# Decay rows of two mixers: spread by DMA through DRAM and formed on GpSimd, instead of by matmuls on TensorE

## The reference

```python
# first block: state space mixer, 16 heads (chunks of 64 in the reference)
seg = a_cs[..., :, None] - a_cs[..., None, :]          # a_cs: running sum of dt * a
decay = exp(where(causal, seg, -inf))
y = (cb * decay) @ (x * dt)                            # cb = C B^T, per group of 8 heads
# beside it a gated linear recurrence, both gated, projected, then an FFN
# second block: gated delta rule, 4 heads, chunks of 64
diff = gc[..., :, None] - gc[..., None, :]             # gc: running sum of g in a chunk
L = (beta k) k^T * exp(diff)   (strictly lower);   a_qk = q k^T * exp(diff)   (lower)
qg = q * exp(gc);   d_last = exp(gc at the chunk's end)
# beside it three more branches (spatial gate, sliding window, memory), merged by gates
```

## Time and profile before

| what | value |
|---|---|
| median of three runs | 1000.08 us (998.61 to 1000.84) |
| the profiled execution | 1000.26 us, of it span 998.5 us |
| TensorE busy | 95% of the span |
| VectorE, ScalarE, GpSimd busy | 62%, 50%, 44% |
| mean granted clock of TensorE | 0.966 |
| DMA | 143.37 MB, 44% of the 16 engines' time |

### The profile page before, as it was taken

One profiled execution on the slowest core, in us unless ns is written; L12 is line 12 of the kernel. 1 busy time (PEld: TensorE's weight loads), 2 busy tenths in 40 slices (PEclk: granted clock), 3 DMA queues, 4 the chain that ended last, 5 costly groups with the idle time before them and its releaser, 6 DMA issues.

```text
span 998.5 us, 17155 instructions
## 1 busy us (share of the span) xinstructions
PE 945.6 (95%) x6754; PEld 877.0 (88%) x6754; DVE 619.4 (62%) x1160; ACT 502.4 (50%) x784; POOL 434.6 (44%) x344
## 2 busy tenths in 40 slices
PE   6879999989998999999997989999999999999995
PEld 6879988979997999999996989999999777778884
DVE  6797644966867855645557787653656543655564
ACT  5556667645343755656554557333445423445541
POOL 3444222557363665565554424221322322445652
PEclk9999999979997999999999999998999989999998
DMA  8435432436451555565553345432322322346541
GB/s 322 155 122 179 149 107 85 134 120 226 151 179 61 188 189 188 172 189 189 178 183 105 101 145 194 128 108 76 131 85 85 108 84 83 115 147 196 193 151 43
DMA packets 39684, 143.37 MB, mean 144 GB/s; under 512 B 4402, under 2 KB 4532, under 8 KB 39348
## 3 DMA queue, kind: packets, MB, share of 16 engines
q1 hardware_dynamic: 39604, 142.27, 43.6%
HBM read 141.21 MB, written 1.05 MB: 142 GB/s over the span
## 4 chain that ended last, share of the span: by engine, by line
PE 78%; DVE 15%; ACT 4%; issue 2%; POOL 1%; DMA 1%; SPq 0%; ACTq 0%; DVEq 0%
PE bank L535 29%; PE bank L530 16%; PE bank L531 16%; PE bank L532 16%; DVE t_arena L1638 5%; DVE t_wl L1624 3%; DVE t_arena L1630 2%; DVE t_sm L1635 2%; PE bank L538 2%; ACT t_wh L1167 1%; ACT t_arena L1172 1%; DVE t_arena L1844 1%; DVE t_arena L1634 1%; ACT t_br L1172 1%; DVE t_sm L1634 1%
## 5 line engine op out<-in xcount | busy, mean ns | idle before, releaser
L2271 POOL TENSOR_TENSOR t_wl<-t_raw,t_wh 128x384 fp32r<-128x384 f32 x260 | 365.9, 1413 | 489.6 <-ACT t_wh L1167 489.6
L530 PE MATMUL bank<-t_hh,t_wh 128*128 128x256 f32 x1208 | 353.0, 292 | 12.4 <-DVE t_wl L1624 9.0
L531 PE MATMUL bank<-t_hl,t_wh 128*128 128x256 f32 x1208 | 344.6, 285 | 0.0
L532 PE MATMUL bank<-t_hh,t_wl 128*128 128x256 f32 x1208 | 344.4, 285 | 0.0
L1624 DVE TENSOR_TENSOR t_wl<-t_raw,t_wh 128x640 fp32r<-128x640 f32 x260 | 244.6, 946 | 152.3 <-ACT t_wh L1167 151.2
L1167 ACT ACTIVATE t_wh<-t_raw 128x1024 fp32r<-128x1024 f32 x260 | 272.2, 1056 | 129.1 <-PE bank L532 93.9
L530 PEld LDWEIGHTS bank<-t_hh,t_wh 128*128 128x128 f32 x1208 | 234.6, 194 | 17.9 <-DVE t_wl L1624 10.7
L531 PEld LDWEIGHTS bank<-t_hl,t_wh 128*128 128x128 f32 x1208 | 234.8, 194 | 0.3
L532 PEld LDWEIGHTS bank<-t_hh,t_wl 128*128 128x128 f32 x1208 | 234.4, 194 | 0.0
L530 PE MATMUL bank<-t_br,t_wh 128*128 128x256 f32 x424 | 124.8, 294 | 10.7 <-DVE t_br L1638 8.4
L531 PE MATMUL bank<-t_br,t_wh 128*128 128x256 f32 x424 | 123.4, 291 | 0.0
(11 more groups left out here) (139 smaller groups left out, 1023.4 us busy)
## 6 DMA issues: line engine op xcount, KB each, us to landing
t_raw<-in_ws SPq DMA_DIRECT2D x260, 512.0 KB, 4.2
t_x<-in_xin SPq DMA_DIRECT2D x4, 256.0 KB, 5.8
t_bd<-in_bd SPq DMA_DIRECT2D x1, 1024.0 KB, 11.5
t_arena<-in_mem SPq DMA_DIRECT2D x1, 1024.0 KB, 5.0
out<-t_arena SPq DMA_DIRECT2D x4, 256.0 KB, 2.4
t_arena<-in_post SPq DMA_DIRECT2D x1, 512.0 KB, 5.5
t_con<-in_con SPq DMA_DIRECT2D x1, 384.0 KB, 6.5
t_arena<-in_masks SPq DMA_DIRECT2D x1, 320.0 KB, 9.5
```

Of the source, the lines that this page charges most:

```text
L530: e.matmul(o, wh, xh, start=first, stop=False, skip_group_check=True)
L531: e.matmul(o, wh, xl, start=False, stop=False, skip_group_check=True)
L532: return e.matmul(o, wl, xh, start=False, stop=last, skip_group_check=True)
L2271: e.tensor_tensor(WL[q % NS][:, LOW:1024], RAW[q % NR][:, LOW:1024], WH[q % NS][:, LOW:1024].bitcast(F), SUB).then_inc(*lo2.now(q))
```

## The change

The rows no longer go through TensorE. `acs` is written to a DRAM tensor `decay` and read back into all 128 partitions (`ACS`, 16 rows of 256, 2.1 MB in all, in the place of `BR`). GpSimd forms row plus negated column, held at most at zero, for 256 and 128 columns per head, into one of four buffers `DEC`; ScalarE's `Exp` becomes one instruction of 384 columns in place; the causal mask is multiplied into `CBT` once. In the delta rule `beta`, `gc` and `eg` go through `gates2` into `BG` (12 rows of 256, 1.6 MB in all), GpSimd forms differences plus mask, and VectorE reads `BG` where it read PSUM. The four DMAs stand on SP's queue among the fetches. The copies `identR`, `ACR` and the mask `maskS` are gone, `INCL` is made at tick 12 instead of in the second block, and `kk` moves a tick earlier and uses three banks in turn.

```diff
@@ sp_program, in the loop over the fetches q @@
+                if q == 20:
+                    e.wait_ge(*d_dt.of("acs"))
+                    e.dma_start(decay, acs).then_inc(s_decay[0], 16)
+                if q == 23:
+                    e.wait_ge(s_decay[0], 16)
+                    e.wait_ge(*unit.of(LAST["xbc5"]))
+                    e.dma_start(ACS, decay.partition_broadcast(P)).then_inc(s_decay[1], 16)
+                if q == LAST["dnq4"] + 1:
+                    e.wait_ge(*d_rw.of("beta"))
+                    e.wait_ge(*a_rw.of("eg"))
+                    e.dma_start(gates2[0], ROW[0:4, 0, :]).then_inc(s_gates[0], 16)
+                    e.dma_start(gates2[1:3].rearrange("i h t -> h i t"), ROW[4:8, 1:3, :]).then_inc(s_gates[0], 16)
+                if q == LAST["dnq5"] + 3:
+                    e.wait_ge(s_gates[0], 32)
+                    e.dma_start(BG, gates2.rearrange("i h t -> (i h) t").partition_broadcast(P)).then_inc(s_gates[1], 16)
@@ pe_program, ssd_lane @@
-                for h in range(16):
-                    yield from walk.until(T_HEAD + h)
-                    ps = PB[3 + h % 2]
-                    sel = identR[0:16, h:h + 1].to_broadcast([16, 128])
...
-                    mm(ps[:, 0:128], identB[:, :], maskS[:, :], True, False)
-                    for w in range(2):
-                        mm(ps[:, 0:T], sel, ACR[:, w, :], False, w == 1)
-                    mm(ps[:, T:384], identB[:, :], maskS[:, :], True, False)
-                    for w in range(2):
-                        m = mm(ps[:, T:384], sel, ACR[:, w, 128:256], False, w == 1)
-                    m.then_inc(*p_ssd.now("seg", h))
-                    if h % 2 == 1 and h > 1:
-                        y_pair(h // 2 - 1)
-                yield from walk.until(42)
-                y_pair(7)
+                for t in range(8):
+                    yield from walk.until(T_HEAD + 2 * t + 3 - t // 7)
+                    y_pair(t)
@@ pe_program, dn_lane @@
                     yield from walk.until(170 + 2 * h)
-                    for i in range(2):
-                        mm(PB[3][:, 128 * i:128 * i + 128], identB[:, :], maskD[:, :], i == 0, False)
-                    mm(PB[3][:, 0:T], sg, ROW[0:8, 1, :], False, True)
-                    mm(PB[3][:, T:512], sg, ROW[0:8, 2, :]).then_inc(*p_dn.now("seg", h))
-                    mm(PB[4][:, 0:T], sb_, ROW[0:8, 0, :]).then_inc(*p_dn.now("beta", h))
-                    yield from walk.until(171 + 2 * h)
                     for hf in range(2):
                         for w in range(2):
-                            m = mm(PB[5][...], k_[...], (k_, q_)[w][...])
+                            m = mm(PB[3 + h % 3][...], k_[...], (k_, q_)[w][...])
@@ act_program, ssd_lane @@
                 for h in range(16):
                     yield from walk.until(T_HEAD + h)
-                    e.wait_ge(*p_ssd.of("seg", h))
...
-                    act(dec[:, 0:T], ps[:, 0:T], ACT.Exp, bias=cols_dt[:, 2, h:h + 1])
-                    act(dec[:, T:384], ps[:, T:384], ACT.Exp, bias=cols_dt[:, 3, h:h + 1]).then_inc(*a_ssd.now("exp", h))
+                    e.wait_ge(*g_ssd.of("seg", h))
+                    act(DEC[h % 4], DEC[h % 4], ACT.Exp).then_inc(*a_ssd.now("exp", h))
@@ act_program, dn_lane @@
-                    yield from walk.until(171 + 2 * h)
-                    e.wait_ge(*p_dn.of("seg", h))
-                    for hf in range(2):
-                        act(ET[:, hf, h, :], PB[3][:, 128 * hf:128 * hf + 128], ACT.Exp,
-                            bias=ngc[:, hf, 4 + h:5 + h]).then_inc(*a_dn.now("dec", h, hf))
+                    yield from walk.until(169 + 2 * h)
+                    e.wait_ge(*g_dn.of("seg", h))
+                    act(ET[:, :, h, :], ET[:, :, h, :], ACT.Exp).then_inc(*a_dn.now("dec", h))
@@ dve_program, ssd_lane @@
+                tt(INCL[:, :], cn("strict"), ident, ADD).then_inc(*d_const.now("incl"))
                 for g in range(2):
...
-                    e.tensor_copy(CBT[:, g, :], PB[4][:, 0:384]).then_inc(*d_ssd.now("cb", g))
+                    for i in (0, 2):
+                        tt(CBT[:, g, 128 * i:128 * i + 128], PB[4][:, 128 * i:128 * i + 128], INCL[:, :], MUL)
+                    e.tensor_copy(CBT[:, g, 128:256], PB[4][:, 128:256]).then_inc(*d_ssd.now("cb", g))
@@ pool_program @@
+            def ssd_lane():
+                for h in range(16):
+                    yield from walk.until(T_HEAD + h)
+                    if h == 0:
+                        e.wait_ge(s_decay[1], 16)
+                        e.wait_ge(*d_dt.of("cols"))
+                    if h >= 4:
+                        e.wait_ge(*p_ssd.of("y", (h - 4) // 2))
+                    for i, sl in enumerate((slice(0, T), slice(T, 384))):
+                        m = e.tensor_scalar(DEC[h % 4][:, sl], ACS[:, h, 128 * i:T], cols_dt[:, 2 + i, h:h + 1], 0.0, ADD, MIN)
+                    m.then_inc(*g_ssd.now("seg", h))
+                yield
+
+            def dn_lane():
+                for h in range(4):
+                    yield from walk.until(168 + 2 * h)
...
+                    for hf in range(2):
+                        e.tensor_scalar(ET[:, hf, h, :], BG[:, 4 + h, 128 * hf:128 * hf + 128], ngc[:, hf, 4 + h:5 + h], None,
+                                        ADD).then_inc(*g_dn.now("diff", h, hf))
+                    for hf in range(2):
+                        e.wait_ge(*g_dn.of("diff", h, hf))
+                        m = tt(ET[:, hf, h, :], ET[:, hf, h, :], maskD[:, :], ADD)
+                    m.then_inc(*g_dn.now("seg", h))
+                yield
+
+            walk.lanes = [ffn_lane(), ssd_lane(), lru_lane(), rows_lane(), dn_lane()]
```

More of the change, by code:

```diff
@@ L142, in constants @@
     return [np.concatenate([out[n] for n in names], 1).astype(np.float32)
-            for names in ([n for n, _ in CON], ("ssm", "sw", "seg"))]
+            for names in ([n for n, _ in CON], ("sw", "seg"))]
 class Tally:
@@ L290, in dn_bank, with build_program @@
     return 3 + (DN_AT[name] + 1) % 3
-def build_program(nc, ws, par, con, masks, bd, rows, swt, xin, min_, post2, out):
+def build_program(nc, ws, par, con, masks, bd, rows, swt, xin, min_, post2, decay, gates2, out):
     ctx = ExitStack()
@@ L313, in build_program @@
         s_sp, s_out, s_post = sem("s_sp"), sem("s_out"), sem("s_post")
+        s_decay, s_gates = [sem(f"s_decay{i}") for i in range(2)], [sem(f"s_gates{i}") for i in range(2)]
         s_x = [sem(f"s_x{i}") for i in range(4)]
@@ L344, in build_program @@
         NW2 = SM[:, 352:364].rearrange("p (a b) -> p a b", a=3)
-        maskS = sb("maskS", [P, 128], BF)
         maskW = sb("maskW", [P, 384], BF)
-        maskD = sb("maskD", [P, 128], BF)
+        maskD = sb("maskD", [P, 128])
         identB = sb("identB", [P, 128], BF)
-        identR, ACR = sb("identR", [P, P], R), sb("acr", [16, 2, T], R)
         INCL = sb("incl", [P, P], BF)
         PX, PW = sb("px", [P, 1024]), sb("pw", [P, 768])
-        MSK = ar(0, 640)
+        MSK = ar(0, 512)
         XBC = ar(0, 12, T)
@@ L365, in build_program @@
         CBT = ar(76, 2, 384)
-        DEC = ar(79, 3, 384)
+        DEC = [ar(79, 384), ARENA[:, 79 * 256 + 384:79 * 256 + 768], ar(82, 384), ar(88, 384)]
+        ACS = BR.rearrange("p a b -> p (a b)").bitcast(F).rearrange("p (h t) -> p h t", h=16)
+        BG = ar(78, 12, T)
         DTR = ar(84, 4, T)
@@ L695, in ssd_lane @@
                 e.wait_ge(*d_rs.of("ssd"))
-                e.wait_ge(*a_ssd.of("exp", 15))
+                e.wait_ge(*d_ssd.of("cb", 1))
                 for g in range(2):
@@ L1239, in ssd_lane @@
                 act(DTR[0:16, 1, :], DTR[0:16, 1, :], ACT.Exp, scale=-1.0).then_inc(*a_dt.now("exp"))
-                yield from walk.until(12)
-                e.wait_ge(*d_dt.of("acs"))
-                act(ACR[:, 0, :], acs, ACT.Copy).then_inc(*a_dt.now("acr"))
                 for h in range(16):
                     yield from walk.until(T_HEAD + h)
-                    ps, dec = PB[3 + h % 2], DEC[:, h % 3, :]
-                    e.wait_ge(*p_ssd.of("seg", h))
-                    if h == 0:
-                        e.wait_ge(*d_dt.of("cols"))
-                    if h >= 3:
-                        e.wait_ge(*p_ssd.of("y", (h - 3) // 2))
-                    act(dec[:, 0:T], ps[:, 0:T], ACT.Exp, bias=cols_dt[:, 2, h:h + 1])
-                    act(dec[:, T:384], ps[:, T:384], ACT.Exp, bias=cols_dt[:, 3, h:h + 1]).then_inc(*a_ssd.now("exp", h))
+                    e.wait_ge(*g_ssd.of("seg", h))
+                    act(DEC[h % 4], DEC[h % 4], ACT.Exp).then_inc(*a_ssd.now("exp", h))
                 yield from walk.until(43)
@@ L1414, in act_program @@
             h_parts("mix", SC1)
-            e.wait_ge(s_con, 16)
-            act(identR[:, :], ident, ACT.Copy).then_inc(*a_const.now("identR"))
             def gates(i):
@@ L1777, in ssd_lane @@
```

(13 more changed lines are left out.)

44 lines of the change are left out of this document (20 added, 24 removed).

## The result

The changed kernel is slower: 1019.02 us (median of 4 runs, 1012.23 to 1022.73) against 1000.46 for the kernel before beside it, a ratio of 1.018 with a 95% interval of 1.0125 to 1.0237. Timed a second time it came to 1016.41 against 998.07, 1.0192 (1.0168 to 1.0216). The prediction of 1002.7 had the direction, and its range ended at 1010: 9 us too early.

The account below looks back on a forecast made before the run. TensorE, busy for 95% of the span, was taken as the bound, with ScalarE and GpSimd taking turns in the mixer after the change. +10.3 - 6.8 + 0.8 - 1.7 = +2.6 us gave 1002.7 us, range 994 to 1010.

Parts of the forecast that it names:

- The loop: Mixer, each unit: high part, GpSimd's low part, differences, Exp, next high part wait in a closed ring; 5.56 us a unit.
- x: Mixer: time of GpSimd's two difference instructions per head, taken as 0.9 us, ends 0.62 and 1.25.
- +10.3: Mixer: total lateness in us summed over all heads, arriving at `gsum`; ends +6.1 and +15.5.
- some 3 us less: Mixer: how much the sum would fall at the skill page's best GpSimd rate, 0.58 us for 384 columns.
- the 17.8 us: Mixer: row matmuls taken from TensorE, 16 x 1.11 us, said to become idle time in front of the units.
- The start after the high part (0.08) and the low part (1.48): Mixer: hand-over from ScalarE's high part to GpSimd, 0.08 us, and mean time of GpSimd's low part, 1.48 us.
- The exclusion that the Trainium skill states: Mixer: two-SBUF-input VectorE instructions and GpSimd ones reading SBUF exclude each other; cited for the 1007.9 us rival, chance 0.2.
- `decay`: Copy through DRAM ahead of unit 23's fetch: hidden, cost 0, up to 2 us at the slow end.
- `gates2`: Gates' copy on SP's queue ahead of unit 168's fetch, waiting for `eg`: +0.8 us, ends 0 and 2.3.
- Delta rule: Four heads: 6.8 us of row matmuls saved, plus 1.7 us from one avoided clock fall (ends 0 and 5.0).
- The clock in the mixer: Rival: gaps lower TensorE's clock in the mixer, 7.1 us a unit, 22 us more, 1025 us; chance 0.06.
- The loop does not bind: Rival: in the mixer TensorE's time is won, heads 0 to 10 end 12 us earlier, 982 us; chance 0.07.

Follow-up runs that it names:

- thin differences: Changed kernel, but from head 4 on GpSimd forms only 2 columns per difference instruction and Exp has scale 0: 1004.79 us, ratio 1.0052.
- the mixer alone: Kernel before with only the mixer's part of the change, the delta rule left as it was: 1024.92 us, ratio 1.024.
- delta rule's part alone: Kernel before with only the delta rule's part of the change, gates' copies placed as in the change: 994.5 us, ratio 0.9953.
- GpSimd ahead: Changed kernel with GpSimd forming the mixer's differences one tick earlier, at tick 24+h: 977.95 us, ratio 0.9785.
- late copies: Kernels with the gates' writes and broadcast moved to 4 and 7 units behind dnq5; with differences a tick earlier 975.4 us, delta rule's part only 991.21 us.

## Why the prediction was wrong, by its own steps

**The loop: right. x: wrong, and it is nearly the whole miss.** The step that failed reads "I take x = 0.9, nearest to the casts", with 1.25 as the upper end. Measured: 1.83 undisturbed, and 2.69 and 2.68 beside VectorE's scans and low part (the pairs at 196.96 and 209.18 us). The 15 pairs of heads 1 to 15 add up to 29.2 us, where the sum has 15 x 0.9 = 13.5: 15.7 us more than the +10.3, 26.0, where the trace has 25.9 at `gsum` and 24.7 at unit 54. It holds in parts:
- Heads 0 to 11 take 71.1 us from `Exp` to `Exp` (112.01 to 183.12), 6.46 us each; 5.56 + 0.93 is 6.49.
- Head 11 to 12 takes 11.3 us against 9.25: +2.0, forecast +1.05 with an x too small by 0.93.
- Heads 12 to 14 take 12.2 against 6.47: +5.8, forecast +3.2 with two such x, of which one is too small by 0.94 and the other, beside the scans, by 1.79: +5.9.

Put into the same sum, the pairs of the thin differences give 26.0 - 14.8 = 11.2, where `gsum` came 11.2 us later and unit 54 10.3. So the mechanism of the forecast was right and one term of its sum was not. Its ends were taken from casts (of the three casts of 128 columns in that trace, 344, 478 and 877 ns, the shortest) and from a subtraction split in two, and neither is a bound for this operation: with one input it costs more than the two-input one, 1139 ns for 256 columns against a mean of 733 for `t_x<-t_x,t_arena` of the same width in the kernel before. Undisturbed, the difference between 256 and 128 columns is (1139 - 712) / 128 = 3.3 ns a column, and two columns take 0.29 us, nearly all of it fixed time. The Trainium skill (GPSIMD Engine Reference, 3.1) gives 1.8 cycles an element at best and 2.6 for a two-input addition. The 3.3 ns are more than both: at the 1.2 GHz of that section, an estimate, 4.0 cycles. The prediction's "some 3 us less" from the best rate does not come out of its own numbers either: 15 x (0.9 - 0.58) is 4.8.

**That the loss "arrives at `gsum`, for which TensorE waits already", and that the 17.8 us turn into idle time:** right. The loss of the mixer alone stays at +25.4 to the end.

**The start after the high part (0.08) and the low part (1.48):** right: 0.08 (114.21 to 114.29), and 1.48 on average from 110 to 190 us.

**The exclusion that the Trainium skill states (SBUF — State Buffer, Who interferes with whom):** the trace agrees at the low part, 1.65 us at 114.29 with VectorE's beside it against 1.03 at 195.95, and in the thin kernel, where two columns took 0.99 us instead of 0.29 while VectorE's low part of 0.82 us ran (136.03 us). Of the pairs of differences only two met such work (2.7 against 1.83), since VectorE waited for `Exp` as well: none up to head 12, 1.7 us of the miss in all.

**`decay`:** forecast 0 and right. The broadcast took 10.4 us to land, between my 5 and 17, the fetch of unit 23 behind it landed at 83.0 us, 2 us ahead of its high part, and units 23 to 30 are within 1 us of before in every kernel that has it.

**`gates2`:** forecast +0.8, ends 0 and 2.3; measured +5.6, +5.1 (delta rule's part alone) and +5.3 (GpSimd ahead), and 3.3 to 4.0 in the other four profiles with early copies (3.3 in the second one of the changed kernel). The wait was named rightly, and with it the late fetch. Two terms were missed. The loads of `swt` and `rows` stand at the same place of the same queue and put the fetch of 168 another 1.1 us back. And that fetch, the first of four issued together, landed 6.3 us after its issue and not 3 to 4.2. In the seven profiles its landing takes 4.05, 4.3, 4.5, 4.7, 5.8, 6.0 and 6.3 us, and the loss is 3.3, 3.6, 3.8, 4.0, 5.1, 5.3 and 5.6: the one follows the other. Why the landing varies so was not tried.

**Delta rule:** -6.8 for the row matmuls and -1.7 for the clock, 8.5; measured -9.5 to -9.6 in three profiles with this part (the first of the changed kernel among them) and -11.0 in eight. The three have one fall of the clock of 3.4 us left in the stage, the eight none, where the kernel before has 10.2 us at the lower level. So 3.4 us at that level cost 1.5, all 10.2 some 4.5, and about 6.5 are left for the matmuls. The step that failed here is "I count the first fall, a third of it, as avoided": two thirds were, or all. Ahead of the stage, from unit 168 to 180, a new fall takes some of it back, which was not forecast: 1.4 us in three of the four kernels with late copies, 0.2 in the changed kernel.

**The clock in the mixer (a rival with 0.06):** it did fall to 0.50, at gaps of 4.9 to 7.3 us, and set nothing: from 110 to 215 us ScalarE never waits for TensorE, and the loop alone accounts for the shift. The idle time was forecast as gaps of 1.6 us a unit, in front of most units; that was wrong. Until 190 us it comes in three pieces (7.3, 5.4 and 4.9 us), because TensorE's next task behind its lead is the recurrent unit's matmul, which waits for ScalarE's tanh and exp, queued behind the waiting `Exp`.

**The rivals.** "The loop does not bind" was given 982 us. The true one is beside it: the loop need not exist. I took the order of GpSimd's program as given, weighed whether it binds, and did not ask what one tick would change. Sum of the terms as measured: 24.7 + 1.2 + 5.6 - 9.5 = 22.0, and the span's difference is 22.4 us. The profiled execution is the slowest of its four; by the medians the difference is 18.6. The second profile has a shift of 16.2 at the end: 2.3 less at the fetch of 168, and 1.5 less in the delta rule and 1.7 less behind it, each with one fall of the clock fewer.

## What to carry to other kernels

Where an engine is given new work, write down for each unit what stands ahead of what in its program and in that of its partner: two engines that wait for each other within a unit add their times, and one tick of lead makes them overlap. Price such work by a row with the same operation; a cast or a copy is no price for arithmetic on GpSimd, and a two-input addition was none for this one-input form. Where there is no such row, the upper end has to lie well above the nearest ones. Before a transfer is put on a queue that also feeds the stream, list everything else that stands at that place, and what the transfer waits for.

## What the runs showed of the hardware

- GpSimd, fp32: arithmetic with a column operand and two operations takes 1139 ns for 128x256, 712 for 128x128 and 293 for 128x2, undisturbed. A pair of 256 and 128 columns: 1.83 us; without the second operation 1.50; with two constants 1.67; as a copy 0.63.
- The same pair of copies took 1.43 us while VectorE ran its scans, and the pair of differences 2.69 beside scans and low part.
- A DMA that reads 16 KB of DRAM into each of 128 partitions (2 MB) landed in 10.4 to 12.1 us, one of 12 KB in 8.5 to 13.1. The issue of the latter held SP's queue for 0.65 to 1.81 us right behind four fetches, and for 0.42 us at its later place.
- TensorE's clock fell to 0.50 within a gap of 7 us (125.4 to 132.7 us) and was full again some 4 us after work came back. A fall of 3.4 us cost 1.5 us in the delta rule. From unit 192 to 258, where the kernel before has 13.7 us at the lower level, profiles with 10.2 us gain 1.5 to 1.7 us on it, those with 3.4 us gain 4.7, and those with 20.5 us lose 3.1.
